# Stick-breaking attention placed inside the query and key projections, after the value projection

## What is computed

```
def stick_breaking_attention(h, w_qkv, w_o):
    q, k, v = jnp.split(h @ w_qkv, 3, axis=-1)          # 16 heads of 128
    for i in range(s // BLOCK_Q):                        # 2 blocks of 128 queries
        z = jnp.einsum('bqhd,bkhd->bhqk', q[:, lo:hi], k[:, :hi]) * scale
        log_1m_beta = jnp.where(causal, jax.nn.log_sigmoid(-z), 0.0)
        tail = lax.cumsum(log_1m_beta, axis=3, reverse=True) - log_1m_beta
        a = jnp.where(causal, jnp.exp(jax.nn.log_sigmoid(z) + tail), 0.0)
        outs.append(jnp.einsum('bhqk,bkhd->bqhd', a, v[:, :hi]))
    return o @ w_o
x = x + stick_breaking_attention(rmsnorm(x, sb_norm_g), sb_w_qkv, sb_w_o)
```

## Time and profile before

| what | before |
|---|---|
| median of 3 runs | 4307.65 us (4305.82 to 4308.01) |
| span of the profiled execution | 4305.6 us |
| instructions in it | 49124 |
| PE busy | 4156.2 us (97%) |
| DVE busy | 2155.4 us (50%) |
| ACT busy | 1777.0 us (41%) |
| POOL busy | 1027.0 us (24%) |

### The profile page before, as it was taken

The page is one execution under the profiler, slowest core; times in us unless marked ns, Lnnn a source line. Parts: engine busy times, 40 slices in busy tenths (PEclk is TensorE's granted clock), DMA queues, the critical chain, the costliest instruction groups (busy, mean ns, idle before and its releaser), DMA issues.

```text
span 4305.6 us, 49124 instructions
## 1 busy us (share of the span) xinstructions
PE 4156.2 (97%) x20142; PEld 3426.9 (80%) x20142; DVE 2155.4 (50%) x2991; ACT 1777.0 (41%) x2124; POOL 1027.0 (24%) x454
## 2 busy tenths in 40 slices
PE   7997899999999999999989899999999999999998
PEld 6876788877788888888867678887778888888886
DVE  4444478555544444444445646865554444444444
ACT  4344434334444444444443343443334444444443
POOL 1223266111112222222211015631111122222221
PEclk9998999988899999999988899998889999999999
DMA  4550455455575666666643144544557666666664
GB/s 178 184 186 33 163 181 206 157 171 171 166 230 210 239 237 234 234 234 235 238 143 129 67 156 160 203 176 150 167 168 220 215 216 252 235 234 234 229 241 166
DMA packets 279152, 823.25 MB, mean 191 GB/s; under 512 B 146064, under 2 KB 178832, under 8 KB 195216
## 3 DMA queue, kind: packets, MB, share of 16 engines
q1 hardware_dynamic: 94176, 682.73, 44.6%
q10 hardware_dynamic: 184752, 137.38, 10.1%
HBM read 750.84 MB, written 69.21 MB: 190 GB/s over the span
## 4 chain that ended last, share of the span: by engine, by line
PE 94%; DVE 3%; issue 1%; ACT 1%; POOL 1%; DMA 0%; DVEq 0%; SPq 0%; POOLq 0%; ACTq 0%
PE bank L1172 29%; PE bank L1171 14%; PE bank L1315 11%; PE bank L1313 11%; PE bank L1311 11%; PE bank L1282 3%; PE bank L1283 3%; PE bank L1192 3%; PE bank L1194 3%; PE bank L1193 3%; PE bank L1174 1%; DVE lo L687 1%; PE bank L1208 1%; DVE act_t L713 0%; PE bank L1233 0%
## 5 line engine op out<-in xcount | busy, mean ns | idle before, releaser
L435 ACT ACTIVATE hi<-raw 128x1024 fp32r<-128x1024 f32 x1294 | 1368.4, 1059 | 2063.8 <-PE bank L1172 1059.6
L687 DVE TENSOR_TENSOR lo<-raw,hi 128x1024 fp32r<-128x1024 f32 x887 | 1091.9, 1232 | 1734.4 <-ACT hi L435 1732.8
L1172 PE MATMUL bank<-act_t,hi 128*128 128x512 f32 x5120 | 1869.8, 411 | 5.5 <-DVE act_t L713 5.5
L399 POOL TENSOR_TENSOR lo<-raw,hi 128x1024 fp32r<-128x1024 f32 x407 | 985.6, 2422 | 3204.3 <-ACT hi L435 3204.3
L1171 PE MATMUL bank<-act_t,lo 128*128 128x256 f32 x4800 | 1404.2, 293 | 0.0
L1172 PEld LDWEIGHTS bank<-act_t,hi 128*128 128x128 f32 x5120 | 987.6, 197 | 223.7 <-DVE act_t L713 6.7
L1171 PEld LDWEIGHTS bank<-act_t,lo 128*128 128x128 f32 x4800 | 958.2, 200 | 19.2
L1315 PE MATMUL bank<-hi,wa 128*128 128x512 f32 x2048 | 643.2, 395 | 0.0
L1311 PE MATMUL bank<-hi,wa 128*128 128x512 f32 x2048 | 643.2, 395 | 0.0
L1313 PE MATMUL bank<-lo,wa 128*128 128x512 f32 x2048 | 643.1, 395 | 0.0
L1315 PEld LDWEIGHTS bank<-hi,wa 128*128 128x128 f32 x2048 | 383.9, 187 | 94.0
(11 more groups left out here) (210 smaller groups left out, 2339.6 us busy)
## 6 DMA issues: line engine op xcount, KB each, us to landing
raw<-in_stream SPq DMA_DIRECT2D x647, 1024.0 KB, 4.8
act_rows<-stage ACTq DMA_DIRECT2D x64, 512.0 KB, 3.9
w_rows<-w_stage ACTq DMA_DIRECT2D x64, 512.0 KB, 5.1
acts<-act_rows ACTq DMA_DIRECT2D x64, 512.0 KB, 4.1
w_part<-w_rows ACTq DMA_DIRECT2D x64, 512.0 KB, 5.4
x_res<-in_x SPq DMA_DIRECT2D x2, 1024.0 KB, 6.0
keys_sb<-in_keys ACTq DMA_DIRECT2D x2, 1024.0 KB, 4.8
out<-xn SPq DMA_DIRECT2D x2, 1024.0 KB, 4.0
```

The lines of the kernel that those rows point to most:

```text
L399: pool.tensor_tensor(lo[:, s, :], raw[:, n0 % RAW_SLOTS, j * HALF:(j + 1) * HALF], hi[:, s, :].bitcast(F32), ALU.subtract).then_inc(lo_rea ...
L435: act.activation(hi[:, s, :], raw[:, slot, j * HALF:(j + 1) * HALF], ACT.Copy).then_inc(hi_ready[s], 1)
L687: dve.tensor_tensor(lo[:, s, :], raw[:, n0 % RAW_SLOTS, j * HALF:(j + 1) * HALF], hi[:, s, :].bitcast(F32), ALU.subtract).then_inc(lo_read ...
L1172: ins = mm(ps[:], w_hi, act_t[:, kt, :, :].rearrange("p w t -> p (w t)"), start=first, stop=last)
```

## The change

The value projection goes first. The query and key units of one head are put side by side in the stream (unit 2h is q of head h, 2h+1 is k of head h), and `qk_t` is laid out to match. The loop over heads is now a loop over slots: slot h holds the two units of head h. In the middle of the q unit PE makes the scores of head h-1 and the later sums of head h-2; in the middle of the k unit it makes the output of head h-3. Three steps are left after slot 15; they go whole into the middles of the first three wo units, which PE's list begins one by one, each waiting for the four heads that it reads. The scores and the outputs get banks of their own (4 and 5) and semaphores of their own; the outputs go to a new tensor `ot_t`, in the place of `qk_t`, in place of `act_t`. DVE, ACT and POOL get lists to match, in which the splits of units 2h+2 and 2h+3 (`slot_unit(h, 0)` and `slot_unit(h, 1)`) stand between the steps. No matmul, no activation and no vector operation is added or left out. The core of it:

```
-PHASE_UNITS = [("qk", 32), ("v", 16), ("wo", 16), ("wq0", 16), ("peer0", 2 * TILES),
+PHASE_UNITS = [("v", 16), ("qk", 32), ("wo", 16), ("wq0", 16), ("peer0", 2 * TILES),
...
+        def slot_unit(h, second):
+
+            if h < HEADS:
+                return U0["qk"] + 2 * h + second + LEAD
+            return None if second else U0["wo"] + h - HEADS + LEAD
...
+            split_range(0, U0["qk"] + LEAD)
+            for h in range(HEADS + TAIL):
+                split_lo(slot_unit(h, 0))
+                if 2 <= h < HEADS + 2:
+                    mask_head(h - 2, st_e, st_a, 2, st_exp, head_full, 0, st_weights)
                 if h < HEADS:
...
+                    split_lo(slot_unit(h, 1))
+                if 1 <= h < HEADS + 1:
+                    mask_head(h - 1, st_sp, st_spm, 3, st_soft, c_full, C0["stick"], st_masked)
```

ACT's list:

```
+            for h in range(HEADS + TAIL):
+                split_hi(slot_unit(h, 0))
+                if 1 <= h < HEADS + 1:
+                    g = h - 1
+                    tmp = st_l[:, g % 2, :]
+                    act.wait_ge(score_free, g + 1)
...
                     steps.sync()
                     act.activation(tmp, tmp, ACT.Ln, bias=1.0).then_inc(st_log, 1)
...
+                if 2 <= h < HEADS + 2:
+                    g = h - 2
                     act.wait_ge(st_args, g + 1)
...
+                if h < HEADS:
+                    split_hi(slot_unit(h, 1))
+                if h >= 3:
+                    g = h - 3
+                    act.wait_ge(head_full, g + 1)
+                    act.activation(ot_t[:, g, 0, :], ps_head[:, 0:S], ACT.Copy).then_inc(ot_hi, 1)
```

DVE's list (`score_args` holds the operations of L1019 and L1023, `less_tail` that of L1028, `softplus` those of L1037 and L1039):

```
+            for h in range(HEADS + TAIL):
+                split_lo(slot_unit(h, 0))
+                if 1 <= h < HEADS + 1:
+                    score_args(h - 1)
+                if 2 <= h < HEADS + 2:
+                    less_tail(h - 2)
                 if h < HEADS:
...
+                    unit_done(dve, U0["qk"] + 2 * h)
+                    sum_halves(qk_t[:, h, 0, :], A0["qk"] + 2 * h)
+                    split_lo(slot_unit(h, 1))
+                if 1 <= h < HEADS + 1:
+                    softplus(h - 1)
                 if h < HEADS:
...
+                    unit_done(dve, U0["qk"] + 2 * h + 1)
+                    sum_halves(qk_t[:, h, 1, :], A0["qk"] + 2 * h + 1)
+                if h >= 3:
+                    g = h - 3
+                    dve.wait_ge(ot_hi, g + 1)
+                    dve.tensor_tensor(ot_t[:, g, 1, :], ps_head[:, 0:S], ot_t[:, g, 0, :].bitcast(F32),
+                                      ALU.subtract).then_inc(head_free, 1)
```

PE's list:

```
+            def scores(g):
+                pe.wait_ge(a_free, GRANTED + A0["qk"] + 2 * g + 2)
...
+            def later_sums(g):
...
+                pe.wait_ge(st_masked, g + 1)
...
+            def head_out(g):
+                if g >= 1:
+                    pe.wait_ge(head_free, g)
+                pe.wait_ge(st_weights, g + 1)
+                head_outputs(ps_head, g, v_tok, st_a[:, g % 2, :], head_full)
...
+            for h in range(HEADS):
+                unit_a(U0["qk"] + 2 * h, A0["qk"] + 2 * h, middle=lambda h=h: slot_first(h))
+                unit_a(U0["qk"] + 2 * h + 1, A0["qk"] + 2 * h + 1, middle=lambda h=h: slot_second(h))
+            pe.wait_ge(b_free, B0["wo"] + 1)
+            for u in range(4):
+                pe.wait_ge(head_free, 4 * u + 4)
+                tokens_by_columns(U0["wo"] + u, ps_b[B0["wo"] % 2], ot_t, 4 * u, KT,
+                                  middle=(lambda h=HEADS + u: slot_whole(h)) if u < TAIL else None)
+            pe.wait_ge(score_free, HEADS)
+            for nb in range(1, 4):
+                block_b(U0["wo"] + 4 * nb, B0["wo"] + nb, ot_t, 4)
```

More of the change, by code:

```diff
@@ L608, in _ @@
             act.activation(cos_t[:].rearrange("p c f -> p (c f)"), ang[:, 5, :], ACT.Sin).then_inc(trig, 1)
-            split_range(LEAD, U0["wo"] + LEAD)
+            split_range(LEAD, U0["qk"] + LEAD)
             act.preload_act_table_set("natural_log_exp_and_others")
[L613 to L619, removed]
+            for h in range(HEADS + TAIL):
[4 more added lines that the diff above has]
+                    act.wait_ge(score_free, g + 1)
+                    if g >= 2:
+                        act.wait_ge(st_soft, g - 1)
+                    steps.do(act.activation(tmp, st_arg[:, g % 3, :], ACT.Abs))
                     steps.sync()
@@ L1004, in _ @@
             dve.wait_ge(trig, 2)
[L1005 to L1008, removed]
             blocks(U0["v"], B0["v"], 4, lambda idx, col, last: copy_block(idx, v_tok, col, last))
-            for h in range(HEADS + OUT_LAG):
-                if h < HEADS:
[L1014 to L1033, removed]
-                if h < HEADS:
-                    steps.sync()
-                    dve.wait_ge(st_log, h + 1)
-                    dve.tensor_tensor(sp_, sp_, st_l[:, h % 2, :], ALU.add).then_inc(st_soft, 1)
-                    dve.wait_ge(st_soft, h + 1)
-                    steps.do(dve.tensor_tensor(arg, arg, sp_, ALU.subtract))
@@ new lines, in less_tail, with softplus @@
+            def less_tail(g):
+                older = st_arg[:, g % 3, :]
+                steps.sync()
+                dve.wait_ge(c_full, C0["stick"] + g + 1)
+                dve.tensor_tensor(older, older, ps_c[(C0["stick"] + g) % 2][:, 0:LIVE],
+                                  ALU.subtract).then_inc(st_args, 1)
+                dve.wait_ge(st_args, g + 1)
+                dve.sem_inc(c_free, 1)
+            def softplus(g):
+                sp_, arg = st_sp[:, g % 2, :], st_arg[:, g % 3, :]
+                steps.sync()
+                dve.wait_ge(st_log, g + 1)
+                dve.tensor_tensor(sp_, sp_, st_l[:, g % 2, :], ALU.add).then_inc(st_soft, 1)
+                dve.wait_ge(st_soft, g + 1)
+                steps.do(dve.tensor_tensor(arg, arg, sp_, ALU.subtract))
@@ L1180, in unit_a, with tokens_by_columns @@
                 weights_by_features(n0, ps_a[idx % 2], middle)
-            def tokens_by_columns(n0, pair, act, kt0, kt_end, width=512, k_tiles=2):
+            def tokens_by_columns(n0, pair, act, kt0, kt_end, width=512, k_tiles=2, middle=None):
                 for j, s, k in halves(n0):
                     pe.wait_ge(lo_ready[s], k + 1)
+                    if j and middle:
+                        middle()
                     for q in range(k_tiles):
@@ L1365, in _ @@
-            pe.wait_ge(b_free, GRANTED + B0["stick"] + HEADS)
-            for nb in range(4):
-                block_b(U0["wo"] + 4 * nb, B0["wo"] + nb, act_t, 4)
+            def scores(g):
+                pe.wait_ge(a_free, GRANTED + A0["qk"] + 2 * g + 2)
+                if g == 0:
+                    pe.wait_ge(b_free, GRANTED + B0["v"] + 4)
+                else:
+                    pe.wait_ge(score_free, g)
+                qh, kh = qk_t[:, g, 0, :], qk_t[:, g, 1, :]
+                mm(ps_score[:, 0:S], kh[:, 0:P], qh, start=True, stop=True)
+                mm(ps_score[:, S:LIVE], kh[:, P:S], qh[:, P:S], start=True, stop=True).then_inc(score_full, 1)
@@ new lines, in head_out, with slot_first, slot_second @@
+            def head_out(g):
[3 more added lines that the diff above has]
+                head_outputs(ps_head, g, v_tok, st_a[:, g % 2, :], head_full)
+            def slot_first(h):
+                if 1 <= h < HEADS + 1:
+                    scores(h - 1)
+                if 2 <= h < HEADS + 2:
+                    later_sums(h - 2)
+            def slot_second(h):
+                if h >= 3:
+                    head_out(h - 3)
```

99 lines of the change are left out of this document (44 added, 55 removed).

## The result

| what | before | after |
|---|---|---|
| median of 8 runs each | 4307.77 us | 4319.74 us (4316.24 to 4321.8) |
| profiled execution, span | 4305.6 us | 4318.9 us |
| PE busy | 4156.2 us | 4169.3 us |
| DVE busy | 2155.4 us | 2184.0 us |
| PE stands still for the attention | 90.24 - 52.10 = 38.1 us | 38.7 us |

What follows compares the result with a forecast made beforehand. PE was taken to bound the kernel, by its stops and slow clock. New terms 35.2 + 31.5 + 10.0 + 11.5 + 4.1 = 92.3 us against 93.1 old gave 4305.6 - 0.8 = 4304.8, say 4305 us; range 4280 to 4328 us.

Steps and rivals of the forecast that it cites:

- work moved into slots: Attention matmuls of 16 heads, 2.2 us each at full clock, stay as PE work: 35.2 us.
- stall at the scores: PE waits 2.1 us for DVE's sum_halves in slots 2 to 16: 31.5 us (19.5 to 45).
- tail, three waits: In the three steps after the last slot, PE waits 5.0, 2.1 and 2.9 us: 10.0 us (8 to 13).
- clock in the slots: Pauses of 1.95 us make the clock fall in 0.45 of 15 slots, 1.7 us each: 11.5 us (0 to 25).
- clock in the tail: Clock falls after the tail's three pauses of 5.0, 2.1 and 2.9 us: 4.1 us.
- sum, against 93.1 of old: New terms total 92.3 us; old is the 90.24 us attention stage plus 2.85 for cold wo units; gain 0.8 us.
- The bound: PE is busy 97% of the span, so only its stops and slow clock can be won back; at most 57.9 us.
- the moves at no cost: Putting v units first, breaking up units, and their loads and splits, was claimed to cost nothing visible.
- Rival 1: The clock holds through the slots' pauses, so 11.5 us are not paid: 4293 us; chance 0.22.
- Rival 2: DVE and POOL do not block each other: stall 1.3 us, no clock fall, 4280 us; chance 0.11.
- Rival 3: DVE's difference wins the port, POOL's mask is last: stall 3.0 us, clock falls in most slots, 4328 us; chance 0.22.
- Rival 4: No overlap, each slot waits for a head's full chain: stalls of 4 us and more, 4335 us; chance 0.05.

Runs made afterwards that it cites:

- e3_pool_order: Changed kernel with one swap in POOL's list: the mask stands before the split of the k unit's successor; 4268.56 us.
- e1_units_moved: Kernel before with only the units moved (v first, q and k of a head side by side), attention still its own stage; 4306.5 us.
- e5_fill8: Changed kernel with 8 needless matmuls in PE's pause at the scores, in the middle of the q unit; 4299.98 us.
- e10_after_sums4: Changed kernel with 4 needless matmuls behind the later sums of slots 2 to 15; 4321.0 us.
- e11_after_sums8: Changed kernel with 8 needless matmuls behind the later sums of slots 2 to 15; 4331.11 us.
- e13_arena_aligned: Changed kernel with POOL's mask before its split and the tail's splits behind the attention's operations, plus the whole arena moved up 32 bytes; 4211.3 us.
- e6_fill4: Changed kernel with 4 needless matmuls in PE's pause at the scores, in the middle of the q unit; 4300.49 us.
- e2_dve_order: Changed kernel with one swap in DVE's list: softplus stands before the split of the k unit's successor; 4292.78 us.
- e7_longer_slot: Changed kernel with 4 needless matmuls in the k unit of slots 2 to 15, at the head of slot_second; 4307.26 us.
- e4_both_orders: Changed kernel with POOL's mask before its split and also DVE's softplus before its split of the k unit's successor; 4271.64 us.

## Why the prediction was right or wrong

The account of the change, term by term (us):

| term | predicted | measured |
|---|---|---|
| work moved into slots | 35.2 | 35.2 (a slot of 13.48 in e3_pool_order is 2 x 5.64 + 2.2) |
| stall at the scores | 15 x 2.1 = 31.5 | 29.5 |
| tail, three waits | 5.0 + 2.1 + 2.9 = 10.0 | 4.6 + 1.9 + 2.7 = 9.2 |
| clock in the slots | 15 x 0.45 x 1.7 = 11.5 | 14 x 1.7 = 23.8 |
| clock in the tail | 4.1 | 2.9 (two falls; 1.1 us of them lie in the pauses) |
| sum, against 93.1 of old | 92.3 | 100.6 |

**What was right.** The bound (PE, by its stops and its clock), the moves at no cost (e1_units_moved), the order inside a slot and the cause of the stall. The prediction gave POOL's split a start 1.2 to 1.4 us after the slot's, DVE's difference 2.8 us beside it, and a stall of 2.1; the trace has 2.62 and 1.9. e3_pool_order takes the cause away and the stall is gone. The tail's three waits came where they were named, each within 0.4 us, from the same reading of the lists. The Trainium skill ("SBUF — State Buffer", "Who interferes with whom") gives this as an exclusive turn at a shared port; the trace agrees, 2.62 us beside POOL's 2.39.

**What was wrong.** The step that failed is in the clock's part: "My pause is 1.95 us in the records, between these rows, so I take 0.45 of the slots". The price per fall, 1.7, was about right (1.58 by e5_fill8, 1.65 between the slots of e10_after_sums4), the length of the pause too; the share was not. The price was right by luck in part: the row it was read from, 368.20 to 371.60, is the first half of a fall that lasted 6.8 us. The clock fell after 14 of 15 pauses: all 13 of 1.9 us and the one of 2.69, not the one of 2.16. That is 23.8 - 11.5 = 12.3 us over the term, and it turned a gain of 0.8 into a loss. I had looked for a length that decides, between rows that fell (1.92, 2.46) and one that did not (1.74), and treated the pauses as 15 separate draws. My own rows spoke against it: the stretch 359.65 to 364.50, at 1.00, holds the pause of 2.46 us before 362.11, so the same length fell at 367.02 and not there. And they are nearly one draw, repeated: the slots are alike, the fall lengthens each by the same amount, so each pause meets nearly the same moment. When the moments vary, 4 and 2 of 13 pauses fell (e10_after_sums4 and e11_after_sums8), so 0.45 was no good mean either; but a mean over moments was the wrong number for a loop in any case. The better form would have been none or all, 4293 or 4304.8 - 11.5 + 15 x 1.7 = 4319 us, each with its chance, and not the sum in the middle. That all the pauses agree is read from one execution: three of the eight took 4316.2 to 4316.5 us at a mean clock of 0.954, some 4 us less than the profiled one at 0.952, about what two or three falls cost.

The other part is smaller. The sum of the measured terms makes after 7.5 us longer; up to the first wq0 matmul the trace has it 10.9 longer. Of the difference, 2 us are the wo units, which the prediction had at no cost, and about 1.4 us are not placed. One row of before, and one of after, of 430 to 500 us (count, busy us, mean ns):

```profile
L1192 PE MATMUL bank<-hi,act_t 128*128 128x512 f32 x88 | 34.2, 389 | 0.0
```

```profile
L1233 PE MATMUL bank<-hi,ot_t 128*128 128x512 f32 x101 | 39.9, 395 | 0.0
```

The diff shows that `ot_t` takes the place of `act_t` as the operand that PE loads, and the prediction passed over it as a change of name; e13_arena_aligned shows its cause. And 2.4 us more arise behind, from the first wq0 matmul to the end of the first layer's expert products, with the same instructions, before and after:

```profile
509.77:2208.64 1698.87, 1698.87 (x8261) 1400.76 (x8262) 863.68 (x1152) 706.98 (x771) 427.64 (x177) 0.97 0.60 208
```

```profile
520.69:2222.00 1701.31, 1701.31 (x8261) 1402.53 (x8262) 863.94 (x1152) 707.12 (x771) 427.36 (x177) 0.97 0.60 207
```

The text of the kernel does not differ there, but the clock does: behind the slow start that both have, it falls 29 times in before and 31 times in after, 3.4 us each, though PE is busy all the time. In all, after spends 5.8 us more of it at half speed, which is 2.9 us by the clock against the 2.4 measured. The two falls more come early in the expert layer. These stretches of before and of after begin at the same instruction and are equally long; after gets through fewer matmuls:

```profile
780.00:828.90 48.90, 48.90 (x255) 38.88 (x254) 29.05 (x31) 21.63 (x26) 7.35 (x3) 0.99 0.42 151
```

```profile
790.57:839.47 48.90, 48.90 (x239) 39.35 (x238) 27.83 (x30) 21.11 (x26) 7.35 (x3) 0.90 0.38 132
```

Why the falls begin earlier there in after is open.

**The rivals.** Rival 1 (the clock holds) is what e5_fill8 and e6_fill4 make of it by force: 4300 us measured, 4293 forecast. The Trainium skill's rule behind it ("TensorE: Matmul & The Clock Gate", "HAM oscillation — how this bites in real kernels"), by which only longer pauses than these do harm, is contradicted here: 13 pauses of 1.9 us were each followed by a fall. Rival 2's stall of 1.3 us is e2_dve_order (1.25 in a slot, with no fall). Rival 3's order appeared in e7_longer_slot at under half its price. Rival 4 did not occur: no stall in a slot is over 2.7 us.

## What to carry to other kernels

In a list that an engine works through in order, put the short step that the bounding engine waits for ahead of a long one on an engine that shares a port, and look at what stands behind the instruction that would lose its turn: here two lines swapped on POOL are worth 51 us, while the same swap on DVE as well costs 3. Short pauses that a loop repeats at one distance are closer to one draw of the clock than to many: cost them at none and at all. Where a pause can't be removed, filling part of it with needless matmuls was enough here. And look at the address of what TensorE loads: with its tensor 32 bytes short of a multiple of 128, the 128 x 512 matmuls here were 2.8% slower.

## What the runs showed of the hardware

**Address of the loaded operand.** In the wo units and the expert products the arena's tensor (`ot_t`, `wa`) is the 128 x 128 operand that PE loads, and `hi` or `lo` is streamed. The same 128 x 512 matmul goes every 0.226 us when the loaded tensor begins on a multiple of 128 bytes, and every 0.232 us when it begins 32 bytes short of one (443 and 431 in 100 us). Multiples of 64 that are none of 128 were not tried, nor the streamed operand's address, which stayed as it was.

**The clock and short pauses.** In the profiled executions it fell after none of 13 pauses of 0.97 us (e6_fill4) and none of 28 of 1.2 to 1.3 us (e2_dve_order, e7_longer_slot); after pauses of 1.9 us in 13 of 13 (after), 4 of 13 (e10_after_sums4) and 2 of 13 cases (e11_after_sums8), which differ in the matmuls put between the pauses and so in their distance; and after all four pauses of 2.7 us in the slots of these three and e2_dve_order. A fall brought 1.2 GHz for 3.35 us in the slot shown, and cost 1.58 us a slot by e5_fill8. The clock also falls where PE does not pause at all (0.90 over the 48.90 us of after shown above).

**The port between DVE and POOL.** DVE's 0.56 us became 2.62 beside a split of 2.39 on POOL, and in e4_both_orders DVE's split became 2.04 beside a mask of 1.33 while POOL's next became 3.20. Busy time on these engines contains such standing: 28.6 us of DVE's in the kernel after.
